# Two raw-weight requests and five other steps moved in a one-core hybrid decoder layer

## What is computed

```python
mod = silu(c) @ w_ada + b_ada                  # 1024 -> 6 x 1024: sh1 sc1 gt1 sh2 sc2 gt2
h = rms_norm(x, g_pre_mix) * (1 + sc1) + sh1
hq, hf, hi, hgate, pv, aq, ak, av = split(h @ w_in)          # 1024 -> 2048
mix = concat([hgrn2(hq, hf, hi, hgate), pool(pv), window_attention(aq, ak, av)]) @ w_out
x = x + gt1 * rms_norm(mix, g_post_mix)
h = rms_norm(x, g_pre_ffn) * (1 + sc2) + sh2
gate, val = split(causal_conv3(h @ w_up))                    # 1024 -> 2 x 2816
x = x + gt2 * rms_norm((gelu(gate) * val) @ w_down, g_post_ffn)
```

## Time and profile before

| | |
|---|---|
| three runs, median (range) | 2187.46 us (2186.54 to 2188.07) |
| the profiled execution: its time / its span | 2186.87 us / 2185.2 us |
| PE busy | 2144.3 us (98%) |
| weight loads on PE, DVE, ACT, POOL busy | 79%, 57%, 41%, 14% |
| DMA, mean over the span | 241 GB/s |
| mean granted clock | 0.997 of full speed |

### The profile page before, as it was taken

One profiled execution on the slowest core, in us unless ns is written; L12 is line 12 of the kernel. 1 busy time (PEld: TensorE's weight loads), 2 busy tenths in 40 slices (PEclk: granted clock), 3 DMA queues, 4 the chain that ended last, 5 costly groups with the idle time before them and its releaser, 6 DMA issues.

```text
span 2185.2 us, 32276 instructions
## 1 busy us (share of the span) xinstructions
PE 2144.3 (98%) x12803; PEld 1727.3 (79%) x12803; DVE 1235.6 (57%) x2101; ACT 887.6 (41%) x1871; POOL 297.2 (14%) x183
## 2 busy tenths in 40 slices
PE   7999999999999999999999999999999999999998
PEld 4776778888887778888888778888888877888886
DVE  3577667774767554545455844455455665355544
ACT  4555555545445343222434543322254444222222
POOL 3322377775300000000000000000000000000000
PEclk9999999999999999999999999999999999999999
DMA  9974789999744447667564346676745444766663
GB/s 361 400 281 176 269 312 352 342 361 361 296 171 175 174 175 268 255 265 267 202 240 158 137 154 232 233 266 256 301 157 214 172 171 156 269 253 233 233 242 117
DMA packets 121503, 527.64 MB, mean 241 GB/s; under 512 B 8832, under 2 KB 39818, under 8 KB 70154
## 3 DMA queue, kind: packets, MB, share of 16 engines
q1 hardware_dynamic: 121353, 525.58, 64.5%
HBM read 410.20 MB, written 115.34 MB: 241 GB/s over the span
## 4 chain that ended last, share of the span: by engine, by line
PE 91%; ACT 3%; DVE 2%; DMA 1%; issue 1%; SPq 1%; POOL 0%; DVEq 0%; ACTq 0%; POOLq 0%
PE ps L771 18%; PE ps L773 18%; PE ps L772 18%; PE ps L1224 5%; PE ps L1226 5%; PE ps L1225 5%; PE ps L793 4%; PE ps L795 4%; PE ps L794 4%; PE ps L888 1%; PE ps L832 1%; PE ps L833 1%; PE ps L834 1%; PE ps L935 1%; PE ps L715 1%
## 5 line engine op out<-in xcount | busy, mean ns | idle before, releaser
L771 PE MATMUL ps<-hTh,wt 128*128 128x512 f32 x1792 | 705.5, 394 | 2.0 <-DVE hTl L1819 2.0
L772 PE MATMUL ps<-hTl,wt 128*128 128x512 f32 x1792 | 698.3, 390 | 0.0
L773 PE MATMUL ps<-hTh,wt 128*128 128x512 f32 x1792 | 698.2, 390 | 0.0
L771 PEld LDWEIGHTS ps<-hTh,wt 128*128 128x128 f32 x1792 | 336.6, 188 | 80.9 <-issue 10.8
L773 PEld LDWEIGHTS ps<-hTh,wt 128*128 128x128 f32 x1792 | 336.7, 188 | 71.0
L772 PEld LDWEIGHTS ps<-hTl,wt 128*128 128x128 f32 x1792 | 336.8, 188 | 67.7
L2173 DVE SCALAR_TENSOR_TENSOR cv<-ps,CW,cv 128x511 f32<-128x511 f32 x176 | 131.8, 749 | 413.7 <-ACT cv L1675 413.7
L1675 ACT ACTIVATE cv<-ps,CW 128x510 f32<-128x510 f32 x176 | 136.2, 774 | 555.9 <-PE ps L773 544.5
L662 POOL TENSOR_TENSOR wt<-raw,wt 128x1024 fp32r<-128x1024 f32 x72 | 171.9, 2404 | 261.8 <-ACT wt L1307 261.6
L2144 DVE TENSOR_TENSOR Y<-Y,ps 128x512 f32<-128x512 f32 x192 | 130.2, 687 | 126.6 <-PE ps L1226 126.6
L1224 PE MATMUL ps<-wt,pTh 128*128 128x512 f32 x448 | 174.7, 390 | 1.5 <-issue 1.4
(11 more groups left out here) (317 smaller groups left out, 2840.7 us busy)
## 6 DMA issues: line engine op xcount, KB each, us to landing
wt<-split_w SPq DMA_DIRECT2D x300, 1024.0 KB, 4.8
split_w<-wt SPq DMA_DIRECT2D x100, 1024.0 KB, 7.1
raw<-in_w_up_dram SPq DMA_DIRECT2D x22, 1024.0 KB, 10.8
XT<-in_w_ada_dram SPq DMA_DIRECT2D x10, 1024.0 KB, 12.0
XN<-in_x_dram SPq DMA_DIRECT2D x4, 2048.0 KB, 9.6
raw<-in_w_in_dram SPq DMA_DIRECT2D x8, 1024.0 KB, 14.9
XR<-in_x_dram SPq DMA_DIRECT2D x4, 2048.0 KB, 10.3
XN<-in_w_down_dram SPq DMA_DIRECT2D x16, 512.0 KB, 9.5
```

Of the source, the lines that this page charges most:

```text
L771: mm(ps[:, bank, :], w, hTh[:, k, :], start=(k == 0), stop=False)
L772: mm(ps[:, bank, :], w, hTl[:, k, :], start=False, stop=False)
L773: ins = mm(ps[:, bank, :], wl(slot)[:, k, :], hTh[:, k, :], start=False, stop=(k == KD - 1))
```

## The change

Six places. On SP each `load_in` goes ahead of the modulation set that it followed. On POOL the last difference of a group follows unit q=1's low part, no longer unit q=3's. On PE gate rows 2 and 3 follow unit 2 of the output projection, and the tile-by-tile end takes in unit 5. On ACT the refill of unit 8 follows `take(5)`. On DVE the next block's x is scaled at the end of step i=1.

```diff
@@ sync, first_block
                 free_raw(2)
+                load_in(3)
                 sp.wait_ge(s["ada_mm"], 3)
                 load_set(5)
-                load_in(3)
+                load_in(4)
                 sp.wait_ge(s["prep_tr"], KD)
                 sp.wait_ge(s["ada_mm"], 5)
                 load_set(6)
-                load_in(4)
+                load_in(5)
                 sp.wait_ge(s["ada_mm"], 6)
                 load_set(7)
-                load_in(5)
+                load_in(6)
                 sp.wait_ge(s["ada_mm"], 7)
                 load_set(8)
-                load_in(6)
                 sp.wait_ge(s["ada_mm"], 8)
                 load_set(9)
@@ gpsimd
-                if n in DN_OF and DN_OF[n][1] == 3:
+                if n in DN_OF and DN_OF[n][1] == 1:
                     f = DN_OF[n][0]
                     pool.wait_ge(s["w_lo"], DN_UNIT[f] + 2)
                     pool.wait_ge(s["t_added"], 4 * f + 3)
                     differ(1, 1, 0)
@@ tensor, output projection
-                    if first and u in (1, 3):
+                    if first and u in (1, 2):
...
-                        for i in (u - 1, u):
+                        for i in (2 * u - 2, 2 * u - 1):
                             gate_rows(i)
@@ tensor, last_down and last_down_units
-                        elif u == 6 and last:
+                        elif u == 5 and last:
                             last_down_units()
...
-                    units = [DN_UNIT[LG] + u for u in (6, 7)]
+                    units = [DN_UNIT[LG] + u for u in (5, 6, 7)]
...
-                            for j, k in enumerate(DN_K[2 + i]):
+                            for j, k in enumerate(DN_K[1 + i]):
@@ scalar
-                refill_in(4)
+                if not first:
+                    refill_in(4)
...
                 take(5, UT[:, 1, :]) if first else take_tile(5)
+                if first:
+                    refill_in(4)
                 refill_in(5)
@@ vector, up_step
                     conv(1)
                     if f and i == 0:
                         down(f - 1)
-                    if f == LG and i == 2 and not last:
-                        dve.wait_ge(s["next_r"], b + 2)
-                        for t in range(TT):
-                            ts(XN[:, t, :], XN[:, t, :], rs[:, 0, t:t + 1], None, ALU.mult).then_inc(s["xn_ready"], 1)
...
                     hidden_low(0)
                     hidden_low(1)
+                    if f == LG and i == 1 and not last:
+                        dve.wait_ge(s["next_r"], b + 2)
+                        for t in range(TT):
+                            ts(XN[:, t, :], XN[:, t, :], rs[:, 0, t:t + 1], None, ALU.mult).then_inc(s["xn_ready"], 1)
```

More of the change, by code:

```diff
@@ L1275, in last_down_units @@
                                 mm(ps[:, 4 + t, :], l, w_hi_, start=False, stop=False)
-                                ins = mm(ps[:, 4 + t, :], h, w_lo_, start=False, stop=(i == 1))
+                                ins = mm(ps[:, 4 + t, :], h, w_lo_, start=False, stop=(i == 2))
                             if t == TT - 1:
                                 ins.then_inc(s["unit_done"], 1)
-                            elif i == 1:
+                            elif i == 2:
                                 ins.then_inc(s["tile_done"], 1)
```

## The result

The changed kernel takes **2197.46 us** (median of 6 runs, 2196.62 to 2200.85), the kernel before, run beside it, 2188.06 us (6 runs): a ratio of 1.0046, 95% interval 1.0036 to 1.0056. It is slower, as forecast (2196.0, range 2190 to 2200); by the two medians it lost 9.4 us, for 8.55 forecast. The profiled execution took 2197.63 us with a span of 2195.9, 10.7 more than before.

What follows compares the result with a forecast made beforehand. PE was taken as the bound, busy 2144.3 of 2185.2 us. Terms 9.5 + 2.1 - 0.8 - 1.0 - 1.25 = +8.55 on 2186.87 gave 2195.4, with the median 0.6 higher: 2196.0 us, range 2190 to 2200.

Steps and rivals of the forecast that it cites:

- SP and ACT together, +9.5: First block: set 8 lands later behind more requests, so the level product behind it starts 9.5 us later.
- Stops of 2.3 at set 5, 5 at set 7, near 11 in all: PE waits three times for modulation weights between 60 and 107 us, together near 11 us.
- After set 8 the same bytes have passed; set 9 comes in time.: First block: both request orders have moved equal bytes after set 8, so set 9 is not late.
- L860's stop goes: The 1.9 us stop at 82.11, PE's transposes of V waiting for ACT's take, disappears.
- POOL, +2.1: Down projection, f=0 to 3: the earlier difference holds DVE's L2187 and delays PE, +2.1 us in sum.
- Gate rows, -0.8: Output projection: copies of the gates fall beside unit 3, removing PE's stop before unit 4, -0.8 us.
- x scaled earlier, -1.0: Block 0: DVE scales x before PE wants it, -1.0 us; nothing in blocks 1 and 2.
- The tail, -1.25: Last tile loop: with unit 5 included DVE keeps up and sums the last tile 1.25 us earlier.
- the sets come in time: Rival, first block: engines share time between requests, so sets are not late; 2182.5 or 2181.0 us; chance 0.12.
- DVE isn't held: Rival, down projection: POOL's difference does not hold DVE at its new place; +4.95, 2192.4 us; chance 0.13.
- PE's clock falls too: Rival, first block: PE's stops bring half clock, costing 3.4 us if after set 8; 2199.4 us; chance 0.13.
- Half the delay: Rival, first block: SP gets sets out earlier in some bundles, loss only +5; 2191.5 us; chance 0.07.

Runs made afterwards that it cites:

- e2: Only SP's four moved pair requests, against the kernel before: 2199.57 us, ratio 1.0055.
- e8: Kernel before with only pairs 4 to 6 requested ahead of their sets, pair 3 staying behind set 5: 2195.94 us, ratio 1.0039.
- e10: Changed kernel, but PE multiplies modulation sets 5 to 8 each one unit later: 2190.93 us, ratio 1.0015 to the kernel before.
- e5: Kernel before with only pair 3 requested ahead of set 5: 2189.24 us, ratio 1.0011.
- e1: Changed kernel with SP's order of before put back, the five other edits kept: 2185.17 us, ratio 0.9988 to the kernel before.
- e7: Kernel before with all edits but SP's, POOL's difference also waiting for DVE's sums and first low part: 2181.73 us, ratio 0.9972.
- e3: Kernel before with only POOL's edit: 2188.15 us, ratio 1.0002.
- e4: Kernel before with only pair 6 requested ahead of set 8: 2200.41 us, ratio 1.0053.
- e9: e7 with PE multiplying modulation set 8 after unit 8 instead of unit 7: 2180.43 us, ratio 0.9967 to the kernel before.
- e6: Kernel before with all edits but SP's and POOL's: 2183.77 us, ratio 0.9983.

## Why the prediction was right

The median was forecast 1.5 us too low, and the mechanism is the one forecast. That the sum fits so well is in part luck: several terms are off by half a microsecond to 1.3 us, in both directions. By its steps:

- **SP and ACT together, +9.5.** Measured 10.0 behind set 8. The path is right; its two terms were both off and made up for each other. The bundle was taken as 8.4 us; in the changed kernel set 7's second half landed at 94.3 and pair 6 at 102.1, 7.8 apart, and e2, e8 and e10 have 7.8 to 7.9. The idle start of the new stores was taken as 1.2 us; it is larger. DMA busy tenths from 46 to 58 us, 40 slices of 0.3 us, changed kernel:

```profile
DMA  9999999996300000006899889999999989994975
```

  Before, the same 12 us are full:

```profile
DMA  9999999999998999999999998698999999999999
```

  Seven slices are empty and four beside them partly: about 2.5 us idle, which was the forecast's upper bound, and just what e5 adds to set 8's landing. 7.8 and 2.5 are 10.3; less the 0.2 us that set 8 had to spare, that is the loss. The queue stands still because the stores of units 2 and 3 wait for POOL until 50.8, while what was asked for before has run out at 49.3 already, not at 50. Less the execution's own 0.57, set 5 arrives 1.4 us later than forecast and set 8 0.5.
- **Stops of 2.3 at set 5, 5 at set 7, near 11 in all.** Measured 3.4, 2.7 and 0.33. The sum of the waits was wrong, since half-clock stretches at 68.8 and 96.1 us took their place; the deadline they feed was right.
- **"After set 8 the same bytes have passed; set 9 comes in time."** Right: no wait for a set behind 109 us.
- **L860's stop goes.** Right; and "PE only waits longer" too. That it can be given back even without SP's edit (e1, e7) was not seen: the text said that set 8 had 0.2 us to spare, and did not draw the conclusion that ACT's edit may win nothing by itself. Its first rival and the expectation of e1 count the 1.9 as won.
- **POOL, +2.1.** L2187 is held in turn, 2.48 us at f=0 and 2.50 at f=1: right. At f=0 PE lost 1.4 where 0.8 were forecast: POOL and DVE enter the step 1.0 us later against PE than in before, so PE waits 3.05 us and not 2.1 as in e3; why they do stays open. At f=1 the forecast was 0.75 and PE lost nothing:

```profile
371.10 2.50 DVE L2190 TENSOR_TENSOR P<-P 128x256 f32<-128x256 f32 x1
...
374.44 0.95 DVE L2205 TENSOR_TENSOR pTl<-P,pTh 128x768 fp32r<-128x768 f32 x1
...
375.45 0.49 PE L1224 MATMUL ps<-wt,pTh 128*128 128x512 f32 x1
```

  The low part ends at 375.39 and PE wants it at 375.45: POOL and DVE entered the step 0.5 us earlier against PE than in before. The slack was counted as fixed. f=2 and f=3 cost 0.2 together. Sum about 1.6, near 2.1 with the sizes in the wrong places; that is luck.
- **Gate rows, -0.8.** Measured -1.0, in all kernels with that edit.
- **x scaled earlier, -1.0.** Measured -1.1. The four instructions now stand at 565.97 and last 4.89 us, and PE's transposes at 574.21 wait for nothing:

```profile
565.97 4.89 DVE L2223 TENSOR_SCALAR XN<-XN,rs 128x1024 f32<-128x1024 f32 x4
...
574.21 1.91 PE L849 MATMUL ps<-ident,XN 128*128 128x128 f32 x16
```

- **The tail, -1.25.** Measured -1.27. DVE sums the last tile 0.43 us behind the start of PE's last matmul, for 1.70:

```profile
2188.31 0.39 PE L1276 MATMUL ps<-wt,pTh 128*128 128x512 f32 x1
...
2188.74 0.69 DVE L2161 TENSOR_TENSOR Y<-Y,ps 128x512 f32<-128x512 f32 x1
```

- **Not in the sum.** One stop of 1.0 us in the middle of 64 matmuls that wait for nothing (L948, 137.77), and 0.6 us of small gaps between 239 and 297 us. The first came at the same matmul in e2 (1.22), e8 (1.11) and e4 (0.24), not in e5 or e10, and in no kernel with the old order. The trace names no releaser, and its cause stays open.

Of the rivals, "the sets come in time" fell: the first swap alone makes set 5 late, and e4 makes set 8 late by a pair and its stores. The Trainium skill ("DMA: Bandwidth & Descriptors", section "Queues, rings and completion order") has completion not first-in first-out per engine; no run here shows that: of what was asked for between 37 and 98 us, every set, store and pair landed in the order of issue in all twelve profiles. "DVE isn't held" fell with L2190. The Trainium skill ("SBUF — State Buffer", section "Who interferes with whom") states that a DVE instruction with two SBUF inputs contends with a GpSimd instruction that reads SBUF; the trace agrees, with 2.48 us for 0.43, and e7's 0.42 with POOL elsewhere is the counter-test. "PE's clock falls too" came true twice in the changed kernel and cost little, because both falls lay ahead of set 8, as the prediction said of a fall after set 7. That none came behind set 8, as in e4 and e10, is luck for the number. "Half the delay" fell.

## What to carry to other kernels

In this saturated queue the place of a request was its arrival: 3 MB of other traffic moved ahead of a set made it land some 10 us later, 2.5 of them from the pause that the new order opened. Ask which deadline comes last, for it decides nearly alone: the last of the four swaps costs most of what all four do, and winning time ahead of the deadline can win nothing (e1) until the deadline itself moves (e9). Before an idle engine is given work at an earlier place, look at who uses the same memory at that moment; a wait of one line turned a loss of 1.4 us in time (e1 against e6) into a gain of 2.0 (e7 against e6).

## What the runs showed of the hardware

- Stops of PE ahead of 109 us and the half clock that came with them or right behind: 1.25 and 2.15 us, then 3.4 us (changed kernel, 68.8); 1.30 and 1.41, then 6.8 us (96.1), while nearly the same stops in e2 brought 3.4 us (97.4); 3.69 us in e4 and 2.83 in e8 went with 10.2 us (from 100.6 and 87.5), 2.26 and 1.65 in e10 too (104.2). The 1.59 and 1.46 us of e5 and the 1.71 us at L860 of before brought none, the 3.30 us at L860 of e4 brought 3.4 us. At f=0 there is no fall behind the changed kernel's 3.05 us, and 3.4 us of it behind 2.1 to 2.3 us in e3, e1 and e10. The Trainium skill ("TensorE: Matmul & The Clock Gate", section "HAM oscillation — how this bites in real kernels") tells of a kernel in which the wait for DMA re-throttles PE every time; by these rows many stops do and some do not, and the length of the stop alone does not tell which.
- A fall costs only where it is behind the last deadline: 6.8 us of it ahead of set 8 in the changed kernel and 10.2 in e8 are nearly free, 10.2 us reaching behind it cost 1.8 us in e4 and 3.1 in e10.
- PE's work at 37 us, which no edit reaches, starts up to 3 us apart in these executions (-1.4 to +1.5 against before), though the first matmuls lie within -0.3 to +0.5. The five that are 1.1 to 1.4 us early show 3.4 us of half clock between 27 and 37 us, before and the five at +0.2 to +0.9 show 6.8; e2, the latest, is an exception, with 3.4. With the old order and the transfers as the deadline, an edit of 1.9 us showed in the late one (e6) and not in the early ones (e1, e7).
- A DVE sum of 128x256 took 2.48 to 2.52 us beside a POOL instruction of 128x1024 and 0.42 to 0.43 without; in e7 DVE's low part of 128x1024 took 3.36 us for 1.23, and the POOL low part behind the difference 3.38 for 2.42.
